# Gates of an expert layer scattered once per token with a moving border, one-hots scaled on ScalarE

## The reference, cut to what matters

```
s  = einsum('thpd,hpkd->thpk', (h @ w_q), subkeys)       # 256 tokens, 8 heads, 2 x 128 keys
s1, i1 = top_k(s[:, :, 0], 16);  s2, i2 = top_k(s[:, :, 1], 16)
sc, ci = top_k(s1[..., :, None] + s2[..., None, :], 16)  # 16 of 256 sums per head
expert = i1[ci // 16] * 128 + i2[ci % 16]                # one of 16384 experts
g   = softmax(sc)
act = gelu(h . u_tab[expert]);   y = sum(g * act * v_tab[expert])
```

## Time and profile before

| what | value |
|---|---|
| median of the runs | 2322.8 us |
| profiled execution, span (the page gives no other time of it) | 2329.5 us |
| TensorE matmul busy | 2168.4 us, 93%, 17092 instructions |
| VectorE busy | 1646.3 us, 71% |
| ScalarE busy | 1037.1 us, 45% |
| scatter matmuls, line 1147 | 2048 instructions, 262.7 us busy, 277 ns each |
| one-hots, lines 865, 867, 870 | 106.7, 174.8 and 106.6 us |
| mean granted TensorE clock | 0.965 |

### The profile page before, as it was taken

How to read it: one execution, slowest core, us unless ns; L and a number is a source line. 1 busy time by engine, 2 the same in 40 slices (tenths; PEclk the granted TensorE clock), 3 DMA queues, 4 the chain that set the end, 5 groups by cost and what they waited for, 6 DMA issues and landing times.

```text
span 2329.5 us, 52851 instructions
## 1 busy us (share of the span) xinstructions
PE 2168.4 (93%) x17092; PEld 2090.0 (90%) x17092; DVE 1646.3 (71%) x3922; ACT 1037.1 (45%) x2162; POOL 19.8 (1%) x43
## 2 busy tenths in 40 slices
PE   6778798999999999999999987989999999999998
PEld 5558788999999999999987677889999999999998
DVE  3657998777888655555544589977788886555555
ACT  4334355444333355555544443544443333555554
POOL 1000000000000000000001000000000000000000
PEclk9779999999999899999998999999999998999999
DMA  5203344333443355555552233433334343555553
GB/s 179 73 23 115 115 162 140 106 107 126 138 141 137 116 180 180 183 185 181 182 184 95 71 111 117 162 128 108 108 128 143 136 143 119 183 184 180 180 182 125
DMA packets 90032, 323.57 MB, mean 139 GB/s; under 512 B 9914, under 2 KB 11994, under 8 KB 89728
## 3 DMA queue, kind: packets, MB, share of 16 engines
q1 hardware_dynamic: 88528, 316.71, 39.8%
q0 software_dynamic: 1456, 6.23, 0.8%
HBM read 321.82 MB, written 1.08 MB: 139 GB/s over the span
## 4 chain that ended last, share of the span: by engine, by line
PE 75%; DVE 12%; issue 9%; ACT 2%; DVEq 1%; DMA 0%; POOL 0%; ACTq 0%; POOLq 0%
PE psum L1180 11%; PE psum L1181 11%; PE psum L1182 11%; PE psum L1035 10%; PE psum L1036 9%; PE psum L1037 9%; PE psum L1147 9%; DVE w_lo L603 2%; DVE big L812 1%; ACT w_hi L406 1%; PE psum L1205 1%; DVE big L824 1%; PE psum L1208 1%; DVE big L819 1%; PE psum L1047 1%
## 5 line engine op out<-in xcount | busy, mean ns | idle before, releaser
L603 DVE TENSOR_TENSOR w_lo<-raw,w_hi 128x512 fp32r<-128x512 f32 x1200 | 781.8, 687 | 245.4 <-ACT w_hi L406 242.5
L1035 PE MATMUL psum<-x_hi,w_hi 128*128 128x256 f32 x2752 | 808.9, 294 | 77.9 <-DVE w_lo L603 44.5
L1036 PE MATMUL psum<-x_lo,w_hi 128*128 128x256 f32 x2752 | 785.3, 285 | 0.0
L1037 PE MATMUL psum<-x_hi,w_lo 128*128 128x256 f32 x2752 | 785.2, 285 | 0.0
L406 ACT ACTIVATE w_hi<-raw 128x512 fp32r<-128x512 f32 x1200 | 685.6, 619 | 39.4 <-PE psum L1037 28.8
L1035 PEld LDWEIGHTS psum<-x_hi,w_hi 128*128 128x128 f32 x2752 | 534.8, 194 | 91.1 <-DVE w_lo L603 57.1
L1180 PE MATMUL psum<-ag_hi,w_hi 128*128 128x256 f32 x2048 | 581.9, 284 | 2.9 <-DVE ag_lo L967 2.9
L1181 PE MATMUL psum<-ag_lo,w_hi 128*128 128x256 f32 x2048 | 581.5, 284 | 0.0
L1182 PE MATMUL psum<-ag_hi,w_lo 128*128 128x256 f32 x2048 | 581.4, 284 | 0.0
L1036 PEld LDWEIGHTS psum<-x_lo,w_hi 128*128 128x128 f32 x2752 | 535.5, 195 | 0.0
L1037 PEld LDWEIGHTS psum<-x_hi,w_lo 128*128 128x128 f32 x2752 | 534.1, 194 | 0.0
(11 more groups left out here) (149 smaller groups left out, 1156.5 us busy)
## 6 DMA issues: line engine op xcount, KB each, us to landing
raw<-in_peer_u SPq DMA_DIRECT2D x256, 512.0 KB, 3.2
raw<-in_peer_v SPq DMA_DIRECT2D x256, 512.0 KB, 3.4
raw<-in_peer_q SPq DMA_DIRECT2D x32, 512.0 KB, 3.3
raw<-in_w_qkv SPq DMA_DIRECT2D x24, 512.0 KB, 3.2
raw<-in_w_in SPq DMA_DIRECT2D x16, 512.0 KB, 3.5
raw<-in_w_out SPq DMA_DIRECT2D x8, 512.0 KB, 3.3
raw<-in_w_o SPq DMA_DIRECT2D x8, 512.0 KB, 3.3
big<-bias_scratch POOLq DMA_DIRECT2D x1, 3072.0 KB, 12.1
```

Source lines behind the costliest of these rows:

```text
L603: dve.tensor_tensor(w_lo[:, s, :], raw[:, j % RAW, b * HALF:(b + 1) * HALF], w_hi[:, s, :].bitcast(F32), ALU.subtract).then_inc(split_read ...
L1035: pe.matmul(proj_ps[j % 2], hi, x_hi[:, m, :], start=(m == 0), stop=False)
L1036: pe.matmul(proj_ps[j % 2], hi, x_lo[:, m, :], start=False, stop=False)
L1037: mm = pe.matmul(proj_ps[j % 2], lo, x_hi[:, m, :], start=False, stop=(m == KD - 1))
```

## The change

Each token is scattered once, over all 128 rows, one group per tile, beside tiles 36 to 99 (`FIRST` = 36). When group g is there, tiles up to 36 + g have been taken, so the border moves: VectorE multiplies rows 0 to 36 + g of the four tokens (`rows_done(g)` = 37 + g), ScalarE stores the gates of the rest. Tile 36 + w is taken in two pieces: the tokens of groups already stored (4w of them) go to `fresh` and are multiplied by `gate_partly`, the others go to the table. From tile 100 (`LAST_TURN` = 25) on, whole rows are fresh. The factor of the gate moves from a VectorE multiply over the group to four ScalarE activations with a scale per partition (`scale_hot`). All 64 tiles of the window are written out on ScalarE, VectorE and TensorE. The wait of `apply_gates` is now on `gates_stored`.

```
-LATE_TURN = PICK_TURNS + 8
-LATE = 4 * LATE_TURN
+FIRST = 4 * PICK_TURNS
 GROUPS = T // 4
+LAST_TURN = PICK_TURNS + GROUPS // 4
+LATES = NKEYS - FIRST - 1
+def rows_done(g):
+    return FIRST + g + 1
...
-                def store_gates(k, j):
-                    for half in range(2):
-                        g = 8 * (k - PICK_TURNS) + 2 * j + half
-                        act.wait_ge(scattered, 2 * GROUPS * l + g + 1)
-                        act.activation(table[:, LATE:NKEYS, bass.ds(4 * g, 4)],
-                                       misc_ps[half][:, 0:4 * (NKEYS - LATE)].rearrange("p (t i) -> p i t", t=4), ACT.Copy)\
-                           .then_inc(gates_stored, 1)
-                taking(act_u, take_act, LATE_TURN - PICK_TURNS, k0=PICK_TURNS, besides=store_gates)
+                def scale_hot(g):
+                    act.wait_ge(hot_j_ready, GROUPS * l + g + 1)
+                    for i in range(4):
+                        t, s = 4 * g + i, 4 * (g % 2) + i
+                        mm = act.activation(hot_i[:, s, :], hot_i[:, s, :], ACT.Copy, scale=picks[:, 2, t:t + 1])
+                    mm.then_inc(hot_ready, 1)
+                def take_partly(w):
+                    i = FIRST + w
+                    act.wait_ge(half_used, 2 * (TILE0[act_u] + i) + 2)
+                    if w:
+                        at_least(act, late_gated, LATES * l + w - 2)
+                        act.activation(fresh[:, i % 2, 0:4 * w], proj_ps[i % 2][:, 0:4 * w], ACT.Gelu_apprx_tanh)
+                    act.activation(table[:, i, 4 * w:T], proj_ps[i % 2][:, 4 * w:T], ACT.Gelu_apprx_tanh).then_inc(proj_taken, 1)
+                def store_gates(g):
+                    act.wait_ge(scattered, GROUPS * l + g + 1)
+                    act.activation(table[:, rows_done(g):NKEYS, 4 * g:4 * g + 4],
+                                   misc_ps[g % 2].rearrange("p (t i) -> p i t", t=4)[:, rows_done(g):NKEYS, :], ACT.Copy)\
+                       .then_inc(gates_stored, 1)
+                scale_hot(0)
+                for w in range(GROUPS):
+                    take_partly(w)
+                    ahead(act_u, PICK_TURNS + w // 4, w % 4)
+                    if w + 1 < GROUPS:
+                        scale_hot(w + 1)
+                    store_gates(w)
                 def take_fresh(k, j):
-                    at_least(act, late_gated, (NKEYS - LATE) * l + 4 * (k - LATE_TURN) + j - 1)
+                    at_least(act, late_gated, LATES * l + GROUPS + 4 * (k - LAST_TURN) + j - 2)
                     act.activation(fresh[:, j % 2, :], proj_ps[j % 2], ACT.Gelu_apprx_tanh).then_inc(proj_taken, 1)
-                taking(act_u, take_fresh, NKEYS // 4 - LATE_TURN, k0=LATE_TURN, first=1)
+                taking(act_u, take_fresh, NKEYS // 4 - LAST_TURN, k0=LAST_TURN)
...
-            def one_hots(l, late, g, half):
-                rows = NKEYS - LATE if late else LATE
-                i0 = LATE if late else 0
-                r = 2 * GROUPS * l + (0 if late else GROUPS) + g
-                ahead_of = [picks[:, a_, bass.ds(4 * g, 4)].rearrange("p (t i) -> p t i", i=1) for a_ in range(3)]
-                numbers = iota.rearrange("p (t i) -> p t i", t=1)
-                own_j, own_i = hot_j[:, 4 * half:4 * half + 4, :], hot_i[:, 4 * half:4 * half + 4, 0:rows]
-                at_least(dve, scattered, r - 1)
-                dve.tensor_tensor(own_i, numbers[:, :, i0:i0 + rows].to_broadcast([P, 4, rows]),
-                                  ahead_of[0].to_broadcast([P, 4, rows]), ALU.is_equal).then_inc(hot_step, 1)
-                dve.tensor_tensor(own_j, numbers.to_broadcast([P, 4, P]), ahead_of[1].to_broadcast([P, 4, P]),
-                                  ALU.is_equal).then_inc(hot_step, 1)
-                dve.wait_ge(hot_step, 2 * r + 1)
-                dve.tensor_tensor(own_i, own_i, ahead_of[2].to_broadcast([P, 4, rows]), ALU.mult).then_inc(hot_ready, 1)
-            def apply_gates(l, g, half):
-                dve.wait_ge(scattered, 2 * GROUPS * l + GROUPS + g + 1)
-                early = table[:, 0:LATE, bass.ds(4 * g, 4)]
-                dve.tensor_tensor(early, early, misc_ps[half][:, 0:4 * LATE].rearrange("p (t i) -> p i t", t=4), ALU.mult)\
+            def one_hots(l, g):
+                half = g % 2
+                ahead_of = [picks[:, a_, 4 * g:4 * g + 4].rearrange("p (t i) -> p t i", i=1).to_broadcast([P, 4, P]) for a_ in range(2)]
+                numbers = iota.rearrange("p (t i) -> p t i", t=1).to_broadcast([P, 4, P])
+                at_least(dve, scattered, GROUPS * l + g - 1)
+                dve.tensor_tensor(hot_i[:, 4 * half:4 * half + 4, :], numbers, ahead_of[0], ALU.is_equal)
+                dve.tensor_tensor(hot_j[:, 4 * half:4 * half + 4, :], numbers, ahead_of[1], ALU.is_equal).then_inc(hot_j_ready, 1)
+            def apply_gates(l, g):
+                dve.wait_ge(gates_stored, GROUPS * l + g + 1)
+                early = table[:, 0:rows_done(g), 4 * g:4 * g + 4]
+                dve.tensor_tensor(early, early, misc_ps[g % 2].rearrange("p (t i) -> p i t", t=4)[:, 0:rows_done(g), :], ALU.mult)\
                    .then_inc(act_gated, 1)
+            def gate_partly(l, w):
+                i = FIRST + w
+                dve.wait_ge(proj_taken, PROJ0[f"u{l}"] + i + 1)
+                at_least(dve, gates_stored, GROUPS * l + w)
+                if w:
+                    row = table[:, i, 0:4 * w]
+                    dve.tensor_tensor(row, row, fresh[:, i % 2, 0:4 * w], ALU.mult).then_inc(late_gated, 1)
...
+                one_hots(l, 0)
+                for w in range(GROUPS):
+                    if w + 1 < GROUPS:
+                        one_hots(l, w + 1)
+                    ahead(u, PICK_TURNS + w // 4, w % 4)
+                    if w:
+                        gate_partly(l, w - 1)
+                        apply_gates(l, w - 1)
                 def late_body(k):
                     for j in range(4):
-                        for half in range(2):
-                            one_hots(l, True, 8 * (k - PICK_TURNS) + 2 * j + half, half)
                         ahead(u, k, j)
-                sweep_from(dve, PICK_TURNS, LATE_TURN, late_body, first=0 if l else 1)
-                dve.wait_ge(gates_stored, GROUPS * (l + 1))
-                def early_body(k):
-                    for j in range(4):
-                        g = 4 * (k - LATE_TURN) + j
-                        one_hots(l, False, g, j % 2)
-                        ahead(u, k, j)
-                        if not (isinstance(g, int) and g == 0):
-                            gate_late(l, LATE + g - 1, (j - 1) % 2)
-                        if not (isinstance(g, int) and g < 2):
-                            apply_gates(l, g - 2, j % 2)
-                sweep_from(dve, LATE_TURN, NKEYS // 4, early_body, first=1)
+                        if isinstance(k, int) and k == LAST_TURN and j == 0:
+                            gate_partly(l, GROUPS - 1)
+                            apply_gates(l, GROUPS - 1)
+                        else:
+                            gate_late(l, 4 * k + j - 1, (j - 1) % 2)
+                sweep_from(dve, LAST_TURN, NKEYS // 4, late_body, first=1)
                 gate_late(l, NKEYS - 1, 1)
-                for g in range(NKEYS - LATE, GROUPS + 2):
-                    if g < GROUPS:
-                        one_hots(l, False, g, g % 2)
-                    apply_gates(l, g - 2, g % 2)
...
-                def scatter(late, g, half):
-                    rows = NKEYS - LATE if late else LATE
-                    r = 2 * GROUPS * l + (0 if late else GROUPS) + g
-                    if late:
-                        at_least(pe, gates_stored, GROUPS * l + g - 1)
-                    elif isinstance(g, int) and g < 2:
-                        pe.wait_ge(gates_stored, GROUPS * (l + 1))
-                    else:
-                        pe.wait_ge(act_gated, GROUPS * l + g - 1)
-                    pe.wait_ge(hot_ready, r + 1)
+                def scatter(g):
+                    at_least(pe, act_gated, GROUPS * l + g - 1)
+                    pe.wait_ge(hot_ready, GROUPS * l + g + 1)
                     for i in range(4):
-                        mm = pe.matmul(misc_ps[half][:, i * rows:(i + 1) * rows], hot_j[:, 4 * half + i, :],
-                                       hot_i[:, 4 * half + i, 0:rows], start=True, stop=True)
+                        s = 4 * (g % 2) + i
+                        mm = pe.matmul(misc_ps[g % 2][:, i * P:(i + 1) * P], hot_j[:, s, :], hot_i[:, s, :], start=True, stop=True)
                     mm.then_inc(scattered, 1)
-                def late_body(k):
-                    for j in range(4):
-                        project(u, k, j)
-                        for half in range(2):
-                            scatter(True, 8 * (k - PICK_TURNS) + 2 * j + half, half)
-                def early_body(k):
-                    for j in range(4):
-                        project(u, k, j)
```

(14 more changed lines are left out.)

## The result

| | median | range, runs | ratio to before, 95% interval |
|---|---|---|---|
| before | 2322.95 us | 2320.18 to 2324.05, 4 | |
| after | 2201.59 us | 2201.55 to 2201.83, 4 | 0.9474 [0.9453, 0.9495] |
| forecast | 2185.0 us | range 2177 to 2211 | |

The kernel is 121.4 us faster; 137.6 were forecast. The profiled execution has a span of 2199.9 us and took 2201.62, so 1.7 us lie outside the span. By the same 1.7 the profiled execution of the kernel before (2329.5) was one of some 2331 us, at the slow end of what that kernel does.

A forecast was written before the change was run, and what follows sets the result against it. The prediction took TensorE, busy 93% of the span, as the bound. Savings of 68.3 us in layer 0, 68.1 in layer 1 and 1.2 from the clock make 137.6, so 2322.8 becomes 2185 us, range 2177 to 2211.

The forecast's parts named there:

- Price of the scatter: Scatter on TensorE: 0.111 us per instruction whatever the columns; 512 instead of 1024 per layer, 113.7 us saved in all.
- Window tile 3.767 us: Tiles 36 to 99: each costs what a second-part tile costs now, 3.767 us; 64 make 241.1 us per layer.
- Table load and start stalls: Window: one activation table load per layer; 0.5 us of new stalls and 1.0 us slow clock at layer 0's start.
- ScalarE and VectorE hidden: Window tile: ScalarE's 2.9 us and VectorE's 2.7 to 3.2 us fit behind TensorE's 3.77.
- Rivals A: Window: ScalarE or the gates multiply is not hidden, costing 10 to 26 us, 2195 to 2211; chance 0.10.
- D: Window: a table load stays in every tile, between copy and gelu, +55 us, 2240; chance 0.01.
- E: Window: take, rounding, scaling, scatter, store and multiply become serial; slower, 2343 at a 5.0 us period; chance 0.02.
- Tail 3.9 us: Last projection to combining: combining starts 3.9 us after the last take, not 14.0, with no scatter left.
- Clock at the restart of combining: Combining's start: 3.4 us at the slow clock per layer, giving 1.2 us back over both; bounds -2 and +4.
- The last step of the sum: Whole kernel: the 137.6 us saved is taken from the runs' median, 2322.8, giving 2185 us.
- The 6.7 us between span and median: Kernel before: profiled span 2329.5 us, median of the runs 2322.8, 6.7 lower; the forecast started from the median.
- C: Straight window code: instruction fetch shows as stalls, 0.92 us per four tiles, 29 us, 2214; chance 0.07.

The follow-up runs named there:

- e3: The changed kernel with each scatter matmul over 128 columns cut into two of 64, so twice the instructions; 2314.86 us.
- e2: The changed kernel with the one-hots multiplied by the gate on VectorE again, not by ScalarE activations; 2202.35 us.
- e1: The kernel before, unchanged, run and profiled once more; 2323.03 us, profiled span 2316.8.
- e7: The changed kernel with four idle fp32 matmuls filling TensorE's wait ahead of the first attention scores; 2189.33 us.
- e5: The changed kernel with one idle VectorE reciprocal of 1.75 us added in the norm ahead of attention; 2199.04 us.
- e6: The changed kernel with two idle VectorE reciprocals, 3.5 us, added in the norm ahead of attention; 2196.77 us.
- e11: The kernel before with tiles 36 to 127 written out on TensorE, VectorE and ScalarE in place of loops; 2321.66 us.
- e10: The changed kernel with idle matmuls filling the waits in attention, for the picks and for the norms, not ahead of combining; 2180.59 us.
- e4: The kernel before with only ScalarE's list for tiles 36 to 67 written out in place of its loop; 2308.75 us.

## Why the prediction was right in its mechanism and 16.6 us off

- **Price of the scatter: right.** Forecast 0.111 us an instruction whatever the columns, measured 0.112 at 128 columns in after and 0.112 at 64 in e3.
- **Window tile 3.767 us: right.** Tiles 68 to 99 take 120.54 / 32 = 3.767.
- **Table load and start stalls: right to 0.5 us in layer 0 and 1.2 in layer 1.** 122.58 - 120.54 = 2.0 us were lost in the first part, where 1.5 were allowed, and 1.5 in layer 1, where 2.7 were. The window has one table load per layer:

```profile
L535 ACT ACT_TABLE_LOAD  x2: 1283/1283/1283, 396.8 to 1491.8; - x2
```

- **ScalarE and VectorE hidden: right.** 2.83 us for 2.9, 3.29 for 3.2, and TensorE never waits. Rivals A, D (a load in every window tile) and E (a serial chain) did not come, and by e2 VectorE would have carried the multiply as well.
- **Tail 3.9 us: right** (3.92).
- **Clock at the restart of combining, 1.2 us back: not borne out.** Combining changes by -1.0 us in layer 0 and +0.7 in layer 1, 0.3 us back in all, and with equal fills the changed kernel is 2.1 us slower there. The forecast took the slow stretches of one profile as given; in after the restart is slow for 10.22 x 0.17 / 0.5 = 3.5 us, as estimated (3.4), but combining is as short in e1 (367.5) as in after (367.3).
- **The last step of the sum failed:** "I forecast 2322.8 - 137.6" subtracts two stretches and takes all else as constant, for every execution. The rest is 2201.6 - 655.5 = 1546.1 us after, and 2322.8 - 792.6 = 1530.2 was assumed, 15.9 us less. Attention is the place: 148.9 us, above both values that profiles of the kernel before show (142.6 and 134.0). e7 gives 12.3 us of it back by filling one wait of 1.91 us. The profile of before has a clock of 0.92 in this stage; I had not cut it out, since the change does not touch it.
- **The 6.7 us between span and median** were noted and not followed up. They were the first sign that this program has more than one time, set in the main by a part outside the change.

What stays open: why a wait of 1.91 us brings the clock down in after and not in e1. The two waits are equally long; e5 and e6 show that a shift ahead of it matters, e7 that filling it does. That the moment decides is argued from these and not shown; no run settles it. The 3.8 us between w_o and tile 36 of layer 1 (230.2 in e1 at a clock of 0.97, 234.0 in after at 0.95) was not tried by itself. But e11, with the work of the kernel before, has 234.5 there, also at 0.95, and e10, with the change and the fills, has 229.4, so the change does not cost it.

The forecast by itself stood for 2180 to 2195, and 2201.6 is outside. The range 2177 to 2211 held the time by luck: rivals A and C had stretched it upward, and neither of them happened. What happened was not on the list.

## What to carry to other kernels

Price fp32 matmuls of up to 128 columns that stand back to back by their number: halving the count halved the cost, at about twice the columns in each. At 256 columns the price had doubled (e7). Look at the distances in the place itself, too: in the scores of attention in e7 two matmuls of 128 columns take 0.42 us (from 1183.95 to 1184.37), not 0.22. When a change is worth a few per cent, cut the whole span into stages before and after, the untouched ones too, and read the granted clock of each; profile the old kernel twice, as 13 us of its time may be chance. Where TensorE must wait a microsecond or two, idle matmuls into a free PSUM bank kept the clock up and gave 12.3 us here in one place and 24.7 in all.

## What the runs showed that I had not expected

- A program can settle in an unlucky form: after and e2 have attention at 148.9 us in their profiles, and after's runs spread over 0.3 us; the kernel before spreads over 13 us.
- Adding 1.75 us of work ahead of attention made the kernel 2.6 us faster (e5).
- ScalarE's table load came back in every turn of the loop over tiles 36 to 67, and writing the turns out removed 14 loads of 1.28 us, 7.1 us in each layer (e4). The loop over tiles 68 to 127 has none. The loop over tiles 0 to 35 still has one in each of its nine turns, 18 in after. There four tiles take 13.10 us, where 4 x 2.880 are 11.52 (columns as in the earlier trace rows):

```profile
302.20:315.30 13.10, 12.02 (x96) 11.62 (x96) 12.35 (x36) 6.98 (x14) 0.00 (x0) 1.00 0.51 157
```

  VectorE is busy for 12.35 of the 13.10 us, so by an estimate from this row writing the loop out gives at most 0.75 us a turn, some 13 us over 18 turns. No run tried it.
- Straight code of 92 tiles on three engines cost TensorE nothing to within 0.02 us in each half of its first 64 (e11 against e4, 151.12 to 151.13 and 119.65 in both). The Trainium skill, "Runtime: NRT & Kernel Launch", section "Instruction fetch mechanics", has the crossing of fetch blocks mostly hidden; here TensorE shows none of it.
